# Two column parts of 256 side by side in both MLP products, and joined matmuls in the first one from the seventh job on

## What is computed

```python
h = rms_norm(x, g_mlp) * (1.0 + scale2) + shift2
ff = jnp.square(jax.nn.relu(h @ w_ff1)) @ w_ff2     # 1024 -> 4096 -> 1024
return x + gate2 * ff
```

## Time and profile before

| | |
|---|---|
| median of three runs | 1403.32 us |
| profiled execution | 1403.55 us |
| its span, first to last instruction | 1401.8 us |
| granted TensorE clock, mean | 1.000 |
| busy: TensorE, VectorE, ScalarE, GpSimd | 98%, 58%, 42%, 34% |
| DMA share in 604 to 925 us, and in 925 to 1256 us | 0.38, 0.68 |

### The profile page before, as it was taken

One profiled execution on the slowest core, in us unless ns is written; L12 is line 12 of the kernel. 1 busy time (PEld: TensorE's weight loads), 2 busy tenths in 40 slices (PEclk: granted clock), 3 DMA queues, 4 the chain that ended last, 5 costly groups with the idle time before them and its releaser, 6 DMA issues.

```text
span 1401.8 us, 18026 instructions
## 1 busy us (share of the span) xinstructions
PE 1379.7 (98%) x7332; PEld 1170.7 (84%) x7332; DVE 812.8 (58%) x781; ACT 588.1 (42%) x703; POOL 478.0 (34%) x269
## 2 busy tenths in 40 slices
PE   5999999999999999999999999999999999999998
PEld 3877778898888888888888888888888888888887
DVE  5967688795438974555334453353746434354584
ACT  5667888665325632332222222342322223423152
POOL 0002111145003775574554545531432222333131
PEclk9999999999999999999999999999999999999999
DMA  9444411106210343343433334479997444445552
GB/s 368 170 158 158 155 63 38 46 31 215 116 61 31 120 162 124 137 146 140 152 122 114 127 141 152 166 276 388 377 388 285 151 150 155 167 173 197 200 189 90
DMA packets 75699, 231.27 MB, mean 165 GB/s; under 512 B 5729, under 2 KB 9953, under 8 KB 66786
## 3 DMA queue, kind: packets, MB, share of 16 engines
q1 hardware_dynamic: 75074, 229.60, 44.6%
q10 hardware_dynamic: 544, 0.52, 0.1%
HBM read 165.09 MB, written 65.01 MB: 164 GB/s over the span
## 4 chain that ended last, share of the span: by engine, by line
PE 95%; DVE 2%; DMA 1%; SPq 1%; issue 1%; ACT 0%; POOL 0%; DVEq 0%; ACTq 0%
PE bank L827 19%; PE bank L828 19%; PE bank L829 19%; PE bank L821 9%; PE bank L822 9%; PE bank L823 9%; PE bank L837 5%; PE bank L838 3%; DMA mod_first<-in_w_mod 1%; PE bank L866 1%; PE bank L878 0%; DVE two_r L2194 0%; SPq L590 0%; DVE n_t L2166 0%; PE bank L848 0%
## 5 line engine op out<-in xcount | busy, mean ns | idle before, releaser
L2585 POOL TENSOR_TENSOR w_lo<-w_raw,w_hi 128x2048 fp32r<-128x2048 f32 x28 | 134.7, 4812 | 319.6 <-ACT w_hi L1644 318.1
L2312 DVE TENSOR_TENSOR hin_two<-hin,hin_two 128x3072 fp32r<-128x3072 f32 x28 | 130.3, 4657 | 187.7 <-ACT hin_two L1656 187.7
L827 PE MATMUL bank<-hin_two,w_lo 128*128 128x512 f32 (+1 forms) x576 | 211.4, 367 | 0.0
L828 PE MATMUL bank<-hin_two,w_hi 128*128 128x512 f32 (+1 forms) x576 | 210.8, 366 | 0.0
L829 PE MATMUL bank<-hin_two,w_hi 128*128 128x512 f32 (+1 forms) x576 | 210.5, 365 | 0.0
L1644 ACT ACTIVATE w_hi<-w_raw 128x2048 fp32r<-128x2048 f32 x28 | 53.6, 1915 | 247.3 <-PE bank L838 150.2
L2577 POOL TENSOR_TENSOR w_lo<-w_raw,w_hi 128x512 fp32r<-128x512 f32 x43 | 65.4, 1520 | 183.8 <-ACT w_hi L1582 183.7
L827 PEld LDWEIGHTS bank<-hin_two,w_lo 128*128 128x128 f32 x576 | 108.6, 189 | 18.2 <-issue 0.2
L829 PEld LDWEIGHTS bank<-hin_two,w_hi 128*128 128x128 f32 x576 | 108.6, 189 | 17.7
L828 PEld LDWEIGHTS bank<-hin_two,w_hi 128*128 128x128 f32 x576 | 108.7, 189 | 17.0 <-issue 0.2
L1592 ACT ACTIVATE hid<-bank 128x768 f32<-128x768 f32 (+2 forms) x68 | 52.5, 773 | 162.8 <-PE bank L829 152.6
(11 more groups left out here) (297 smaller groups left out, 3473.5 us busy)
## 6 DMA issues: line engine op xcount, KB each, us to landing
hin<-hid_all SPq DMA_DIRECT2D x28, 1536.0 KB, 6.6
hid_all<-hid SPq DMA_DIRECT2D x105, 384.0 KB, 2.5
w_raw<-in_w_ff SPq DMA_DIRECT2D x36, 1024.0 KB, 9.1
mod_raw<-in_w_mod SPq DMA_DIRECT2D x16, 1024.0 KB, 6.0
w_raw<-in_w_ff SPq DMA_DIRECT2D x60, 256.0 KB, 3.2
x<-in_xT SPq DMA_DIRECT2D x5, 2048.0 KB, 14.3
w_sums<-w_raw SPq DMA_DIRECT2D x8, 1024.0 KB, 15.6
w_raw<-w_sums SPq DMA_DIRECT2D x8, 1024.0 KB, 9.7
```

The source lines that it names most:

```text
L827: pe.matmul(out, w_lo, v_hi, start=first, stop=False, skip_group_check=True)
L828: pe.matmul(out, w_hi, v_lo, start=False, stop=False, skip_group_check=True)
L2312: dve.tensor_tensor(hin_part(n % 3, LO), hin[n % 3][:].rearrange("p t n -> p (t n)"), hin_part(n % 3, HI), ALU.subtract).then_inc(hin_lo_d ...
L2585: pool.tensor_tensor(w2_lo[n % 2][:].rearrange("p t n -> p (t n)"), w2_raw[m % RAWS][:].rearrange("p t n -> p (t n)"), w2_hi[n % 2][:].rea ...
```

## The change

1. The inputs of the first product's part 1 are placed anew: per weight tile 256 columns of the low part and right behind them 256 of the high part (c1_two, t12_two, t4b_two; narrow, narrow_both). Raw values stand where the low part will. ScalarE's modulation of the middle chunk, its high parts and VectorE's sums and low parts of part 1 write and read runs of 256.
2. From the seventh job on (QH = 6) part 1 is done by three_apart, with the whole second bank as result: in columns 512 to 767 of the buffer w_hi·v_lo, in 768 to 1023 the rest. The old reads take columns 0 to 767. VectorE gets eight additions of 256 columns per job (add_low: for P1, P6, P5 ahead of U2, P2 ahead of C11, P7 and P5 again ahead of C22, P3 ahead of C12, P4 behind T2), and then relu and square of B21's part 1 (relu_square) ahead of T4. TensorE waits for ff1_added before P6, P7, P4 (and P2, for the job before). ScalarE's output of P4 is two operations, the narrow one a copy.
3. Each row of hin (one of 4 weight tiles) is 1536 columns now: wide low part, narrow low, narrow high, wide high. So the load writes runs of 3 KB, and both splits are two operations each, a wide and a narrow one. hin2 moves, hin0 takes one piece of 24 KB that overlaps inputs of P6, and its load waits for P6 in the place of P5. ScalarE's split of hin2 loses its wait for all stores.
4. op_lo is one semaphore. A helper of the DFT's matmuls is replaced by an equal one.

```diff
+A_P5, SQ_P4 = 7, 8
+ADDED = (P1, P6, P5, P2, P7, A_P5, P3, P4, SQ_P4)
+QH = REST + 2
...
-    hin_at = (A0 + 98304, A0 + 73728, A0 + 110592)
-    hin_apart = (36864, 12288, 12288)
-    hin = [place(f"hin{i}", [P, GF, HTOK], F32, o) for i, o in enumerate(hin_at)]
-    hin_two = [place(f"hin_two{i}", [P, 2, n // 4], F32R, o) for i, (o, n) in enumerate(zip(hin_at, hin_apart))]
+    hin_at = (A0 + 98304, A0 + 73728, A0 + 122880)
+    hin = [place(f"hin{i}", [P, GF, 2 * HTOK], F32, o) for i, o in enumerate(hin_at)]
+    hin_two = [place(f"hin_two{i}", [P, GF, 2 * HTOK], F32R, o) for i, o in enumerate(hin_at)]
...
+    def hin_both(i, t):
+
+        return hin_two[i][:, t, CH:CH + 2 * QC]
...
+    def added(q, i):
+
+        return len(ADDED) * (q - QH) + ADDED.index(i) + 1
...
             if n < 3:
-                sp.wait_ge(ff1_mm, 7 * (NJ - 1) + (P5, P3, P6)[n] + 1)
+                sp.wait_ge(ff1_mm, 7 * (NJ - 1) + (P6, P3, P6)[n] + 1)
...
-        def three_apart(out, w_hi, w_lo, v, first, last):
-
-            pe.matmul(out.rearrange("p (h n) -> p h n", h=2), w_hi, v, start=first, stop=False, skip_group_check=True)
-            return pe.matmul(out[:, HI * QC:(HI + 1) * QC], w_lo, v[:, HI], start=False, stop=last,
+        def three_apart(out, w_hi, w_lo, v_both, first, last):
+
+            pe.matmul(out, w_hi, v_both, start=first, stop=False, skip_group_check=True)
+            return pe.matmul(out[:, QC:2 * QC], w_lo, v_both[:, QC:2 * QC], start=False, stop=last,
                              skip_group_check=True)
...
             elif i == P2:
                 after(pe, ff1_copy, 4 * q)
+                if q > QH:
+                    pe.wait_ge(ff1_added, added(q - 1, P4))
...
                 pe.wait_ge(ff1_copy, 4 * q + {P6: 1, P7: 2, P4: 3}[i])
+                if q >= QH:
+                    pe.wait_ge(ff1_added, added(q, {P6: P1, P7: P6, P4: P7}[i]))
...
+                both = part == 1 and q >= QH
+                out = ps[:, buf + CH * part:buf + (2 * CH if both else (CH, HTOK)[part])]
                 for kk in range(FT):
...
+                    if both:
+                        m = three_apart(out, w1_hi[o % 4][:, w], w1_lo[o % 4][:, w], narrow_both(i, kk), first, last)
+                        continue
...
+            if i == P4 and q >= QH:
+                act.activation(hid[j][:, CH:HTOK], ps[:, buf + CH:buf + HTOK], ACT.Copy)
+                act.activation(hid[j][:, 0:CH], ps[:, buf:buf + CH], ACT.Relu).then_inc(ff1_copy, 1)
+                act.wait_ge(ff1_copy, 4 * q + 4)
+                act.activation(hid[j][:, 0:CH], hid[j][:, 0:CH], ACT.Square).then_inc(ff1_sq, 1)
+                return
...
+            for part in (WIDE, NARROW):
+                m = act.activation(hin_hi(n % 3, *part), hin_raw(n % 3, *part), ACT.Copy)
+            m.then_inc(hin_hi_done, 1)
...
+        def add_low(q, i):
+
+            own = 2 * (q % 2)
+            buf = {P5: 1, A_P5: 1, P2: 2 - own, P3: 3}.get(i, own)
+            tile = {P1: S_B11, P2: S_B11, P7: S_B22, A_P5: S_B22, P4: S_B21}.get(i, S_T3)
+            part = hid_tile(tile, q)[:, CH:HTOK]
+            if i in (P1, P6, P7, P4):
+                dve.wait_ge(ff1_copy, 4 * q + {P1: 1, P6: 2, P7: 3, P4: 4}[i])
...
+            dve.tensor_tensor(part, ps[:, 2 * CH * buf + HTOK:2 * CH * (buf + 1)], part, ALU.add).then_inc(ff1_added, 1)
...
+        def relu_square(q):
+
+            t = hid[S_B21][:, CH:HTOK]
+            dve.wait_ge(ff1_added, added(q, P4))
+            dve.scalar_tensor_tensor(t, t, 0.0, t, ALU.max, ALU.mult).then_inc(ff1_added, 1)
...
         for q in range(1, NJ):
-            for step in (U2, C11, B11):
+            low = {U2: (P1, P6, P5), C11: (P2,), C22: (P7, A_P5), C12: (P3,)} if q >= QH else {}
+            for step in (U2, C11, B11, C22, B22, C12, B12, T1, T3, T2):
+                if step == C22 and q == NJ - 1:
+                    hin_split_lo(0)
+                for i in low.get(step, ()):
+                    add_low(q, i)
                 hid_out(q, step)
-            if q == NJ - 1:
-                hin_split_lo(0)
-            for step in (C22, B22, C12, B12, T1, T3, T2):
-                hid_out(q, step)
+            if q >= QH:
+                add_low(q, P4)
+                relu_square(q)
```

More of the change, by code:

```diff
@@ L319, in build_encoder, with narrow, narrow_both, modulated @@
     t1_at, t2_at, t12_at, t4_at = X0, X0 + 32768, X0 + 16384, W0 + 24576
[L320 to L325, removed]
+    t1_s, t2_s, t4_s = (place(n, [P, FT, CH], F32, o) for n, o in (
+        ("t1_s", t1_at), ("t2_s", t2_at), ("t4_s", t4_at)))
+    t1_two, t2_two, t4_two = (place(n, [P, 2, FT, CH], F32R, o) for n, o in (
+        ("t1_two", t1_at), ("t2_two", t2_at), ("t4_two", t4_at)))
+    c1_at = (A0 + 8192, A0 + 2 * HALF + 8192)
+    c1_s = [place(f"c1_s{i}", [P, 2, HALF // 4], F32, o) for i, o in enumerate(c1_at)]
+    c1_two = [place(f"c1_two{i}", [P, 2, HALF // 4], F32R, o) for i, o in enumerate(c1_at)]
+    t12_p = place("t12_p", [P, 2, FT * CH], F32, t12_at)
+    t12_two = place("t12_two", [P, 2, FT * CH], F32R, t12_at)
+    t4b_s = place("t4b_s", [P, 2, 4 * QC], F32, t4_at + 16384)
+    t4b_two = place("t4b_two", [P, 2, 4 * QC], F32R, t4_at + 16384)
+    def narrow(tile, ab, part):
+        if tile.shape[2] == 4 * QC:
+            return tile[:].rearrange("p g (f s n) -> p g f s n", f=2, s=2)[:, :, :, part]
+        return tile[:, :, 0:8 * QC].rearrange("p g (f b s n) -> p g f b s n", f=2, b=2, s=2)[:, :, :, ab, part]
+    def narrow_both(i, kk):
+        tile, ab = NARROW_AT[i]
+        row = 2 * QC * (1 if tile.shape[2] == 4 * QC else 2)
+        at = kk % 2 * row + ab * 2 * QC
+        return tile[:, kk // 2, at:at + 2 * QC]
+    NARROW_AT = ((c1_two[0], 0), (t12_two, 0), (t12_two, 1), (c1_two[1], 0), (c1_two[0], 1), (c1_two[1], 1),
+                 (t4b_two, 0))
+    NARROW_S = ((c1_s[0], 0), (t12_p, 0), (t12_p, 1), (c1_s[1], 0), (c1_s[0], 1), (c1_s[1], 1), (t4b_s, 0))
+    def modulated(c, k):
+        if c != 1:
+            return (h2_f, h2_r)[k // FT][:, c, k % FT, :]
+        kk = k % FT
+        rows = c1_s[k // FT][:, kk // 2, 4 * QC * (kk % 2):4 * QC * (kk % 2 + 1)]
+        return rows.rearrange("p (b s n) -> p b s n", b=2, s=2)[:, :, LO]
     def token_sums(i, part):
@@ L466, in build_encoder @@
     op_hi = sem("op_hi")
-    op_lo = [sem(f"op_lo{i}") for i in range(7)]
+    op_lo = sem("op_lo")
     ld_w1 = [sem(f"ld_w1_{b}") for b in range(4)]
@@ L2238, in hid_out @@
             slot, at = [hid_tile(j, q) for j in range(7)], NHID * q
+            if q >= QH and step in (U2, C11, C22, C12, T4):
+                dve.wait_ge(ff1_added, added(q, {U2: P5, C11: P2, C22: A_P5, C12: P3, T4: SQ_P4}[step]))
             if step == U2:
@@ L2311, in hin_split_lo @@
             dve.wait_ge(hin_hi_done, n + 1)
[L2312 to L2313 removed]
+            for part in (WIDE, NARROW):
+                m = dve.tensor_tensor(hin_lo(n % 3, *part), hin_raw(n % 3, *part), hin_hi(n % 3, *part), ALU.subtract)
+            m.then_inc(hin_lo_done, 1)
         def gated(j, dd, o, size, src):
```

89 lines of the change are left out of this document (49 added, 40 removed).

## The result

| | before | after |
|---|---|---|
| median of 7 runs each | 1403.4 us | 1408.65 us |
| lowest and highest | 1403.24 to 1403.6 | 1407.21 to 1409.04 |
| ratio | | 1.0031 [1.0022, 1.0041] |
| profiled execution, its span | 1403.55, 1401.8 | 1407.3, 1405.3 |

1402.5 was forecast, with 1405.6 as the upper end. In some executions of a kernel, and in 4 of the 13 profiled ones here, TensorE's granted clock is 0.50 (its lower level, 1.2 GHz) for one stretch of 3.4 us at about 27 us, which sets all that follows back by some 1.5 us and so shifts a median by as much.

The account below looks back on a forecast made before the run. TensorE, busy 98% of the span, was taken as the bound: number of matmuls times their step. Joined pairs -2.3 plus P4's wait +1.5 gave -0.8 us, 1402.5 us as median; range 1398.2 to 1405.6.

Parts of the forecast that it names:

- Step 1: First product, from the seventh job on: joined pairs replace three 256-column matmuls on 308 tiles, 2.31 us less.
- The 0.027 behind them stays: First product: wide matmuls right behind a run of 8 pairs still lose 0.027 us, as behind 24 narrow ones.
- Step 2: Second product: 320 matmuls read inputs side by side; taken as no gain, bounds 0 and 2.1 us.
- Rival (a): Second product: far-apart input runs do cost TensorE 6.6 ns each, so 4.1 us more gain, 1398.4; chance 0.20.
- Step 3: Each joined job: new VectorE and ScalarE work, 3.8 to 4.8 us, fits; cost 0, covered by the product in between.
- Rival (b): Every joined job: additions come late, P1's at the job's head; half a microsecond beyond costs 5.5 us, 1408; chance 0.10.
- the split hin copies too (some 0.15 us): Splitting hin in two operations costs one more start-up per operation, some 0.15 us, counted within cost 0.
- Step 4: End of last job: hin0's later load delays P7's addition, so TensorE waits some 1.5 us before P4; bounds 0 and 3.
- Step 5: Second product's first steps: later stores delay hin's load, DMA engines full; taken as 0, upper bound 2 us.
- Rival (c): Pairs save nothing (0.36 per tile), or late DMA at the second product's start eats it: 1403.5 to 1405; chance 0.12.

## Why the prediction was wrong

**Step 1, mis-sized.** The pairs cost what the earlier trace rows said, 2.81 against 2.813. "The 0.027 behind them stays" was wrong: it is 0.063, the gain up to 900 is 0.98 us and 1.02 in all, where 2.31 was forecast. I took the price behind a run from a run of other matmuls and from 16 pairs; neither is a run of 8. The gain comes near the 0.8 us that the gap of the Trainium skill (TensorE: Matmul & The Clock Gate, "Back-to-back issue gap") gave, but by chance and not by its way: narrow matmuls still step by 0.113 to 0.120 us, and what was lost is behind the pairs. Not turning the parts round brings 0.7 of it back.

**Step 2, right on its question.** Side by side or far apart is all one to TensorE: 5.64 us for 16 pairs and 16.54 for the period in both, and 113.8 us for the 320 matmuls. Rival (a) is out. The Trainium skill (Advanced Engine Details and Errata, "PSUM Cachelines") says that non-contiguous patterns slow matmuls, and speaks of PSUM; for the input in two far runs, no cost shows here.

**Step 3, right.** 88 additions at 0.42 and no wait in the middle of any of the eleven jobs but the last. Rival (b) didn't happen. But "the split hin copies too (some 0.15 us)" is where a cost was missed: per operation it is 0.07 when nothing is beside it (3.43 against 3.36), and 4.4 when GpSimd comes in between.

**Step 4, right.** 1.39 for 1.5, by the chain described; its links all came about a microsecond earlier than I had put them (hin's low part ended at 920.6 and not 921.8), and TensorE too, so the difference held.

**Step 5, the step that failed.** The term is point 5's "I take 0", with 2 us as its bound. I saw that the stores come later and that the fourth step's half had 0.85 us to spare, but looked for the cost in the DMA alone. It was 2.7, and the engine to look at was VectorE. T4 lasted 5.26 us from 929.47, and the halved subtraction 7.84; with hin as before 0.26 of the loss is left though the stores are as late as ever, with the swapped order about 1.0, and with GpSimd behind T4 0.7. The loss at 991.3 goes nearly or wholly with any of the three, so it can't be shared out between the two places. The number that would have told it stood in rows I had quoted: the relu of 4.42 us beside GpSimd's 4.62, 0.96 alone. I used it as a duration and not as a rule: which of the two starts first decides which is held. In the trace of before T4 was 0.8 us ahead of GpSimd, and the two short operations that the change puts ahead of it (0.79) use that up by themselves.

**The sum.** -0.98 + 1.39 + 2.69 and 0.4 at the end make 3.5 (small steps that add 0.3, and 0.2 less ahead of 604 us, nearly cancel), where -2.3 + 1.5 + 0 was written. Rival (c), "the DMA bound comes true", had the right place and too small a price; no case had the two engines' turns.

## What to carry over

Before moving or splitting an operation of VectorE with both inputs in SBUF, list which long operations of GpSimd start within a microsecond of it, and who is first: its duration is 1 or 5 us by that alone. Where it must be split, put the short piece first. When a saving comes per item and a wait comes once at the last one, leave the last item as it was: ten of eleven jobs keep the gain and none of the wait.

## What the runs showed of the hardware

- An operation of VectorE with both inputs in SBUF that starts during one of GpSimd waits for that one's end. In the traces of before and after, from 455 us on, there are 93 of 768 columns; all end 0.81 to 0.82 us behind GpSimd's, whether that makes them 1.07 or 5.26 us long, and those that meet none take 0.94 to 0.96. If VectorE is first, GpSimd's takes longer by about what VectorE still needs (4.6 becomes 6.06 where VectorE needed 1.57 more). Additions that read one input from PSUM show nothing of it: 73 of 768 columns that start during an operation of GpSimd take 0.94 to 0.96, as the one at 912.13 in the changed kernel in the middle of GpSimd's 4.63 from 911.72.
- The slow steps of 512-column matmuls behind a stream with 256-column ones depend on that stream's length in no simple way: 27 ns in all behind 4 pairs, 63 behind 8, 27 behind 16, 27 behind 24 narrow ones.
- In the kernel whose TensorE stands idle for 4.29 us at the start of the second product, the granted clock is 0.50 behind that (3.41 us, wide matmuls at 0.43 us in place of 0.227), which adds 1.5 us to the wait. Behind the waits of 1.02 to 1.23 us at P4 it stays at 1.00.
- One stretch of 3.4 us at a granted clock of 0.50 at 27 us, behind TensorE's first work, comes in some executions and not in others (the idle time just ahead of it, 1.28 us, is the same in an execution that doesn't have it), and costs 1.5 to 1.6 us.
